# Two sets of operation prices in a scheduler that writes out the engines' order, older ones for the HGRN part

## The reference

```python
# layer 0
h = rmsnorm(x, norm_mix[0])
proj = h @ w_in                       # -> u (256) | q, f, i, g (4 x 768)
pool_out = multi_scale_causal_pool(u) # windows 2/4/8/16, minus self, a linear map per group
f = lb + (1 - lb) * sigmoid(fz); k = (1 - lb) * sigmoid(-fz); v = silu(iz)
S_t = diag(f_t) S_{t-1} + k_t outer v_t;  o_t = S_t^T q_t      # 6 heads, 128 x 128 state
o = o * rsqrt(mean(o*o) + EPS) * gain * sigmoid(gz)
x = x + concat(pool_out, o) @ w_out
x = x + square(relu(rmsnorm(x, norm_mlp[0]) @ ff_w1[0])) @ ff_w2[0]
# layer 1
bg, cg, hv = split(rmsnorm(x, norm_mix[1]) @ odd_w_in)
x = x + (bg * conv3(cg * hv)) @ odd_w_out
x = x + square(relu(rmsnorm(x, norm_mlp[1]) @ ff_w1[1])) @ ff_w2[1]
y = rmsnorm(x, norm_final)
```

## Time and profile before

| | us |
|---|---|
| median of 6 runs | 1518.09 (1514.1 to 1580.4) |
| profiled execution | 1514.85 |
| its span, slowest core | 1513.3 |
| spans of the eight cores | 1497.8 to 1513.3 |
| TensorE busy | 1416.9 (94%) |
| VectorE busy | 1078.6 (71%) |
| ScalarE busy | 849.1 (56%) |
| GpSimd busy | 219.1 (14%) |

### The profile page before, as it was taken

How to read it: one execution, slowest core, us unless ns; L and a number is a source line. 1 busy time by engine, 2 the same in 40 slices (tenths; PEclk the granted TensorE clock), 3 DMA queues, 4 the chain that set the end, 5 groups by cost and what they waited for, 6 DMA issues and landing times.

```text
span 1513.3 us, 25120 instructions; the slowest of 8 cores (1497.8 to 1513.3 us)
## 1 busy us (share of the span) xinstructions
PE 1416.9 (94%) x9189; PEld 710.7 (47%) x9189; DVE 1078.6 (71%) x1911; ACT 849.1 (56%) x1711; POOL 219.1 (14%) x286
## 2 busy tenths in 40 slices
PE   4799799989999898999999999999999999999997
PEld 2555455545445344444445544445544444443442
DVE  4689888777556768867767655557667678867767
ACT  4677668875324546945647422236746546735655
POOL 1134534433300000100100000000000000100100
PEclk9899999999999999999999999999999999999999
DMA  7855145747960534533642322300426535843642
GB/s 162 177 79 80 33 99 100 134 96 174 160 133 15 98 51 75 98 57 70 112 70 43 63 43 51 70 15 1 81 41 104 92 50 97 177 75 70 112 70 112
DMA packets 61715, 130.19 MB, mean 86 GB/s; under 512 B 6350, under 2 KB 33084, under 8 KB 61580
## 3 DMA queue, kind: packets, MB, share of 16 engines
q0 software_dynamic: 25952, 90.78, 37.1%
q1 hardware_dynamic: 34028, 37.48, 8.5%
q10 hardware_dynamic: 1616, 0.33, 0.1%
HBM read 203.86 MB, written 15.54 MB: 145 GB/s over the span
## 4 chain that ended last, share of the span: by engine, by line
PE 67%; DMA 15%; DVE 10%; ACT 4%; issue 3%; ACTq 1%; POOL 1%; SPq 0%; POOLq 0%; DVEq 0%
PE pp L549 43%; PE pp L547 21%; DMA ring<-w2w 7%; DMA ring<-wst 3%; DMA ring<-w1w 3%; PE pp L559 2%; ACT arena L495 2%; DVE arena L514 1%; DVE arena L1680 1%; DVE mixT L514 1%; DVE x_sb L526 1%; DVE x_sb L514 1%; DMA mixT<-xs 1%; DVE ring L514 1%; DMA arena<-st_conv 1%
## 5 line engine op out<-in xcount | busy, mean ns | idle before, releaser
L549 PE MATMUL pp<-hT,ring 128*128 128x512 f16 (+1 forms) x2480 | 463.1, 335 | 15.0 <-DVE ring L514 9.9
L514 DVE TENSOR_TENSOR x_sb<-x_sb,pp 128x512 f32<-128x512 f32 x488 | 321.0, 684 | 120.1 <-PE pp L547 42.1
L549 PEld LDWEIGHTS pp<-hT,ring 128*128 128x128 f16 x2480 | 202.8, 98 | 241.9 <-issue 38.7
L495 ACT ACTIVATE pp<-pp 128x512 f32<-128x512 f32 x336 | 191.6, 583 | 213.6 <-PE pp L547 184.6
L495 ACT ACTIVATE arena<-arena 128x512 f16<-128x512 f16 (+1 forms) x278 | 169.2, 624 | 46.5 <-DVE arena L1680 37.7
L549 PE MATMUL pp<-ring,mixT 128*128 128x512 f16 x824 | 191.9, 379 | 1.7 <-DVE mixT L514 1.7
L495 ACT ACTIVATE arena<-pp 128x512 f32<-128x512 f32 (+5 forms) x228 | 126.8, 562 | 118.6 <-PE pp L549 80.7
L547 PE MATMUL pp<-ring,arena 128*128 128x512 f16 x488 | 125.7, 379 | 0.0
L547 PE MATMUL pp<-hT,ring 128*128 128x512 f16 x448 | 113.2, 379 | 9.7 <-ACT pp L495 9.0
L549 PEld LDWEIGHTS pp<-ring,mixT 128*128 128x128 f16 x824 | 77.7, 98 | 89.9 <-issue 4.4
L564 POOL DMA_DIRECT2D ring<-w2w x56 | 29.5, 529 | 480.3 <-PE pp L549 187.1
(11 more groups left out here) (181 smaller groups left out, 1962.7 us busy)
## 6 DMA issues: line engine op xcount, KB each, us to landing
ring<-wst POOLq DMA_DIRECT2D x57, 512.0 KB, 8.8
ring<-w1w POOLq DMA_DIRECT2D x56, 512.0 KB, 6.6
ring<-w2w POOLq DMA_DIRECT2D x56, 512.0 KB, 6.7
x_sb<-xp SPq DMA_DIRECT2D x28, 512.0 KB, 7.8
yp<-x_sb SPq DMA_DIRECT2D x16, 512.0 KB, 2.7
x_sb<-st_hgrn SPq DMA_DIRECT2D x24, 256.0 KB, 5.8
nhs<-x_sb SPq DMA_DIRECT2D x24, 256.0 KB, 2.5
ring<-wst POOLq DMA_DIRECT2D x8, 256.0 KB, 8.1
```

The source lines that it names most:

```text
L495: return e.activation(out=out, in_=in_, func=func, bias=bias, scale=scale)
L514: return Op(eng, lambda e: e.tensor_tensor(out=out, in0=in0, in1=in1, op=op), R, W, occ, occ + 0.08)
L549: ins = e.matmul(o, l, r, start=s, stop=t)
```

## The change

A list `late` is empty at first; `main` appends to it after the flag `("S", LASTHEAD, 2)`, just ahead of the out projection of the second half. While it is empty, `ACT`, `TT`, `TS`, `STT` and `CP` use older formulas; afterwards those of before. `TT` on GpSimd has the older formula throughout. The three prices of 0.6 us by hand in the seven-product MLP are gone, so that Relu and Square there are priced by `ACT`. No operation is added or taken away by the diff.

```diff
+        late = []
...
-            occ = 0.14 + fsz(in_) / 1280.0 + (0.19 if accum is not None else 0.0)
-            if not in_psum(in_):
-                occ += 0.03
-            if (not isinstance(scale, float) or not isinstance(bias, float)) and fsz(in_) > 8:
-                occ += 0.09
+            n = fsz(in_)
+            if late:
+                occ = 0.14 + n / 1280.0 + (0.19 if accum is not None else 0.0) + (0.0 if in_psum(in_) else 0.03)
+                if (not isinstance(scale, float) or not isinstance(bias, float)) and n > 8:
+                    occ += 0.09
+            else:
+                occ = 0.17 + n / 1400.0 + (0.12 if accum is not None else 0.0)
+                if not isinstance(scale, float) or not isinstance(bias, float):
+                    occ += 0.04
...
-            ps = in_psum(in0) or in_psum(in1)
-            two = not ps and all(a.dtype in (F16, BF16) for a in (in0, in1, out))
-            occ = 0.12 + n / (1925.0 if two else 965.0) + (0.05 if not ps and not two and n > 256 else 0.0)
+            if late:
+                ps = in_psum(in0) or in_psum(in1)
+                two = not ps and all(a.dtype in (F16, BF16) for a in (in0, in1, out))
+                occ = 0.12 + n / (1925.0 if two else 965.0) + (0.05 if not ps and not two and n > 256 else 0.0)
+            else:
+                occ = 0.07 + n / (1920.0 if fast else 900.0)
             if eng == "pool":
-                occ = 0.2 + n / 480.0
+                occ = 0.15 + n / 465.0
...
-            occ = 0.134 + fsz(out) / 1800.0
+            occ = 0.134 + fsz(out) / 1800.0 if late else 0.07 + fsz(out) / 1920.0
...
-            occ = 0.184 + fsz(out) / 964.0
+            occ = 0.184 + fsz(out) / 964.0 if late else 0.1 + fsz(out) / 850.0
...
-            occ = 0.12 + fsz(out) / (1925.0 if eng == "dve" else 465.0)
+            occ = (0.12 if late else 0.07) + fsz(out) / (1925.0 if eng == "dve" else 465.0)
...
-                                yield ACT(v, v, AF.Square, B, B, t=0.6)
+                                yield ACT(v, v, AF.Square, B, B)
...
-                            yield ACT(v, bank(k), AF.Relu, [B_ps[k]], B, t=0.6)
+                            yield ACT(v, bank(k), AF.Relu, [B_ps[k]], B)
...
-                            yield ACT(v, v, AF.Square, B, B, t=0.6)
+                            yield ACT(v, v, AF.Square, B, B)
...
             yield up(("S", LASTHEAD, 2))
+            late.append(1)
             yield from outproj(1, U_WO, 1, "mix", range(8, 17))
```

## The result

The changed kernel takes 1505.7 us (median) against 1517.7 for the kernel before beside it: a ratio of 0.9914, 95% interval 0.9886 to 0.9943. That is 0.9% faster, where 0.3% was forecast, and still inside the 1% called "within". The ratio leaves out executions in which a whole die was granted a lower clock; those in which one or two pairs of neighbouring cores were, at about 0.97 of the full clock over the span, count in it. So I compare stages as means over the eight cores: the mean span goes from 1505.4 to 1499.2 us, which is 6.2 us of the medians' 12.0, as the two profiled executions lie on opposite sides of theirs.

What follows compares the result with a forecast made beforehand. TensorE was taken as the bound nearly everywhere from 212 us on, with VectorE fullest in 112 to 212. 1514.85 + 1.7 - 2.8 - 3.4 + 0 = 1510.4, on the median's scale 1513.6, rounded to 1513; range 1495 to 1535.

Steps and rivals of the forecast that it cites:

- The sign of the whole: Whole kernel: faster, 1513 us forecast against a median of 1518.09, 0.3% below.
- The start was set apart: Before 57 us: the start waits for loads, which no formula of the diff prices, so it was set apart.
- 300 to 352 us, -3.4: Late load of weights costs 6.8 us of idle time and slow matmuls; half counted as gone, -3.4 us.
- 112 to 212 us, -2.8: Order drawn anew; TensorE's idle time falls from 12.6 to 9.8 us, the share of the window before, -2.8 us.
- Hopeful prices, +1.7: HGRN part: unit prices too low by 1.99 us instead of 1.09 put matmuls ahead of their inputs, +1.7 us.
- Rival A: Unit matmuls, 57 to 424 us: hopeful plan makes TensorE stand, +20 us to 1538, idle over 40 us; chance 0.16.
- X and Y at nothing: The two seven-product MLPs: Relu and Square priced 0.05 us too hopeful, taken as 0, bounds +-7 us.
- Rival C: Before 212 us: VectorE meets GpSimd more often, longer means in its rows, +4.5 or +9 us, 1523 to 1527; chance 0.12.
- Rival B: Stops in 112 to 212 and 300 to 352 us go, 20 us faster, 1498; chance 0.22.
- Rival D: Whole kernel: the change does nothing, the order stays unchanged; chance 0.02.

Runs made afterwards that it cites:

- e1: Changed kernel with the three prices of 0.6 us for Relu and Square put back; 1501.8 us, ratio to the kernel before 0.9912.
- s1: Kernel before with the older prices only until the first unit wrote its output, about 44 us; ratio 0.9981, X start 494.1.
- f1: Kernel before, with the slot freed by the out projection given first to head 3's second weights; ratio 0.9976, X start 493.3.
- t3: Changed kernel with the older ScalarE and VectorE prices of the HGRN part times 0.8; ratio to the kernel before 1.0135.
- e2: Kernel before with only the three prices of 0.6 us for Relu and Square taken out; 1518.0 us, ratio 1.0014.
- t2: Kernel before with the scheduler's tie of 0.03 us made 0.04, no price changed; profiled execution 1522.77 us.
- t6: Changed kernel with the prices of 0.6 us put back and the tie of 0.03 us made 0.04; profiled execution 1515.5 us.
- e3: Changed kernel without the switch, so the older formulas hold to the end; ratio to the kernel before 0.9946.
- e4: Kernel before with 0.05 us added to each ScalarE and VectorE price until the switch; ratio 1.0122, X start 514.9.
- t1: Kernel before with the scheduler's tie of 0.03 us made 0.02, no price changed; profiled execution 1529.28 us.

## Why the prediction was right, and where not

**The sign of the whole** was right and the time lies in the range, by a sum that left one term out. It had -4.5 us for the HGRN part; the mean of the cores shows -8.1 at X start, and -11.1 in e1. The signs that it named came: 212 to 300 and 352 to 424 us idle by 1.7 and 2.9% on the slowest core, VectorE's work to 424 us within a few us, X some us earlier, X and Y within 7. But that the sum came near is in part luck. Its terms of 1.7, -2.8, -3.4, 0 and 0 measured 0.7, -0.8, -5.4, -5.4 (the start) and 1.9 (X and Y), and another tie alone moves X by as much as the change does.

**The start was set apart**, because "no formula of the diff prices a load". This step failed. The start also holds ScalarE's squares with a sum, which the older formula prices at 1.02 us for 1024 columns (0.17 + 1024/1400 + 0.12) and the other at 1.16 (0.14 + 0.80 + 0.19 + 0.03), and VectorE's scalings behind them. Their order, not the loads alone, held TensorE at 45.91 us; which of the changed prices moved the scaled block was not tried. The term measured -5.4 us. That 57 to 112 us takes some of it back is not shown: s1, which changes the start alone, loses 7.2 us there for 7.4.

**300 to 352 us, -3.4.** The mechanism was right: the last reader of the slot stood late, and another order freed the slot earlier and had more to do meanwhile. Measured was -5.4 (7.9 to 2.5): the term counted half of a stop that went nearly whole. The earlier slot by itself brought the landing forward by 1.2 us only; what was won is work until then, and the clock that it kept. f1 shows that this stop alone is worth about as much, 4.9 us there.

**112 to 212 us, -2.8.** TensorE's idle time fell from 13.3 to 11.1 us (mean of the cores), near the forecast. The clock was lower, 0.950 for 0.964, and with that the stretch gains 0.8 us. e1, the same order, has 11.7 us idle at 0.964 and gains 1.6, so that the new order holds the clock lower is not shown; either figure is well short of the forecast. The list of TensorE's waits in this stretch has a matmul of a unit at its head, and a pooling step, as in the earlier trace rows, only behind it:

```profile
PE pp L558 <- DVE arena L523: 3.9, 1, 3.9
PE pp L558 <- DVE x_sb L535: 3.7, 3, 1.3
```

The first of these waits ends with a product on VectorE that took 1.25 us where such products have a mean of 0.623, and GpSimd was at work beside it:

```profile
157.20 1.25 DVE L523 TENSOR_TENSOR arena<-arena,gsm 128x384 bf16<-128x384 f32 x1
```

```profile
153.03 5.01 POOL L523 TENSOR_TENSOR x_sb<-x_sb 64x526 f32<-64x526 f32 x4 [8.20 <-DVE arena L523]
```

**Hopeful prices, +1.7.** Measured +0.7 (1.2 to 1.4 and 0.9 to 1.4), but -0.3 in e1, the same order: no cost that stands clear of the spread. **Rival A** asked for over 40 us of idle time from 57 to 424; the slowest core has 23.4. Even the prices of t3, a fifth lower still, come to 36.0 us only (cores 0 to 3).

**X and Y at nothing.** X start to end is the longer part whenever the price by hand is taken out together with measured prices in X: 1008.0 (after), 1009.5 (e2) and 1009.8 us (t3), against 1003.9 to 1007.5 in the seven kernels with `t=0.6` and the old tie, whose mean is 1005.5. Their mean is 1009.1, so that is +3.6 us, inside the bounds of 7 but not nothing. It lies in the last stage: from 565 us after X start to the end these three lose 33.7, 34.2 and 35.3 us, the seven 26.7 to 30.8. The timeline of Y shows a wait of 3.1 us that these three have on all eight cores, and none of the seven on any; after, and then e1 at the same place:

```profile
1262.14 1.38 PE L558 MATMUL pp<-hT,ring 128*128 128x512 f16 x4 [3.09 <-DVE hids L523]
```

```profile
1247.77 1.03 PE L558 MATMUL pp<-hT,ring 128*128 128x512 f16 x4
```

VectorE squares the sample tokens' hidden columns in 0.17 us, but in the new order this stands at 1261.91 behind some dozen block sums:

```profile
1253.79 1.23 DVE L523 TENSOR_TENSOR mixT<-hT 128x2048 f16<-128x2048 f16 x1 [1.11 <-PE pp L556]
...
1261.91 0.17 DVE L523 TENSOR_TENSOR hids<-hids 128x32 f16<-128x32 f16 x1
```

In e1 it stands 12.6 us ahead of that matmul:

```profile
1235.17 0.17 DVE L523 TENSOR_TENSOR hids<-hids 128x32 f16<-128x32 f16 x1
```

The end of VectorE's chain releases TensorE; whether the squares themselves or a block sum just ahead of them is what TensorE needs was not tried. Nor is it tied to these prices (t2 and t6, with the price by hand and the other tie, have one of 3.2 us and rests of 1012.0 and 1010.4), or the whole of the loss: e3 loses 32.9 us in the last stage without it. The new prices also send seven more of the squares to ScalarE (221 from 480 us on, for 214), and no run separates that from the order. The price differences of 0.03 to 0.06 us alone are no more than the prediction said; an order drawn by them is. In the time of the launch this cost is too small to be told apart: e1 and the change have the same ratio.

**Rival C** did not come by the sign that the prediction gave for it. The rows that answer to the earlier trace rows have shorter means, 985 for 1369 ns, 148 for 765 and 147 for 274:

```profile
L535 DVE SCALAR_TENSOR_TENSOR x_sb<-x_sb,cfixw_s 128x512 bf16<-128x512 f32 x4 | 3.9, 985 | 0.0
...
L523 DVE TENSOR_TENSOR dcar<-x_sb 128x1 f32<-128x1 f32 x7 | 1.0, 147 | 0.0
...
L523 DVE TENSOR_TENSOR dcar<-arena 128x1 f32<-128x1 f32 x4 | 0.6, 148 | 0.0
```

Other rows of VectorE lengthened instead, before and after, on all eight cores alike:

```profile
L514 DVE TENSOR_TENSOR gsm<-arena 128x3 f32<-128x3 f32 x4 | 1.3, 322 | 0.0
...
L514 DVE TENSOR_TENSOR hT<-ssq,gcols_s 128x128 f16<-128x128 f32 x1 | 0.3, 292 | 0.0
```

```profile
L523 DVE TENSOR_TENSOR gsm<-arena 128x3 f32<-128x3 f32 x4 | 2.2, 561 | 0.0
...
L523 DVE TENSOR_TENSOR hT<-ssq,gcols_s 128x128 f16<-128x128 f32 x1 | 1.1, 1149 | 0.0
```

So some meetings of the two engines went and others came. An instruction of the same shape takes a fifth of its time when it stands elsewhere, and the neighbour on GpSimd is in the trace: one of the long subtractions of the kernel before ends as GpSimd's product ends, at 153.45 and 153.44 us.

```profile
152.29 1.16 DVE L514 TENSOR_TENSOR dcar<-arena 128x1 f32<-128x1 f32 x1
```

```profile
152.17 1.27 POOL L514 TENSOR_TENSOR arena<-arena 128x512 f32<-128x512 f32 x1
```

That fits the rule of the Trainium skill (SBUF — State Buffer, "Who interferes with whom") that the prediction named, by which the two block each other for a whole instruction; no run here took just the neighbour away. **Rival B** came half: one of its two stretches, 300 to 352 us, runs nearly freely now. **Rival D** is out, as the order changed.

**What was right for the wrong reason.** The prediction asked what prices that are more hopeful do. The runs do not show that, within a few hundredths of a microsecond, the size of the error does anything by itself: closer prices (e4) gave 514.9 us at X start, the older ones 488 to 491, the same ones with another tie 495.0, and the prices of before with other ties 488 on undisturbed cores. The older formulas are not shown to be better; they draw an order without two particular stops. The gain at the start came with them in every run that has them there and no further factor, with the tie of before and in t6 with another (28.7 to 29.7 us lost, 32.8 to 34.3 in the others). The late load also went nearly whole under the prices of before, with another tie in t2 (0.8 us lost).

## What to carry to other kernels

Where a scheduler picks by estimated start, a small change of prices is a new draw of the order: try several, and do not argue that the truer price gives the better order. Look in the profile for the few stops that differ between draws, and mend those by a rule, as the slot rule here did (6.0 us at X start), so that the next edit does not lose them. In a sum of idle times, count the granted clock with each stop, and leave no stage out because the thing it waits for carries no price: the order of what else stands there does.

## What the runs showed of the hardware

In t1 cores 0 and 4 run one order and one program. From about 200 to 350 us core 4 is granted 0.81 of the full clock, window after window, where core 0 has 1.00. Windows of 10 us, core 0 and then core 4:

```profile
180.00:190.00 10.00, 8.66 (x83) 5.50 (x83) 8.66 (x16) 8.49 (x18) 3.54 (x3) 1.00 0.31 109
200.00:210.00 10.00, 9.72 (x84) 5.71 (x82) 7.61 (x15) 7.64 (x16) 0.00 (x0) 1.00 0.31 70
290.00:300.00 10.00, 9.69 (x78) 5.48 (x77) 7.93 (x13) 8.53 (x17) 6.78 (x5) 1.00 1.00 199
```

```profile
180.00:190.00 10.00, 8.71 (x76) 5.18 (x74) 8.69 (x15) 8.65 (x18) 3.54 (x3) 1.00 0.22 71
200.00:210.00 10.00, 10.00 (x53) 4.54 (x52) 7.58 (x17) 5.34 (x12) 0.00 (x0) 0.81 0.39 81
290.00:300.00 10.00, 10.00 (x81) 6.20 (x80) 6.67 (x14) 7.16 (x14) 4.34 (x4) 0.81 0.13 34
350.00:360.00 10.00, 10.00 (x53) 4.36 (x51) 9.96 (x17) 4.47 (x9) 5.74 (x5) 0.90 0.58 173
```

Its neighbour, core 5, shows the same 0.81 from 200 to 210 us, while core 6 of the same die has 1.00; first core 5, then core 6:

```profile
200.00:210.00 10.00, 10.00 (x50) 4.39 (x49) 8.81 (x18) 5.63 (x12) 0.00 (x0) 0.81 0.49 105
```

```profile
200.00:210.00 10.00, 9.95 (x65) 5.00 (x63) 9.14 (x18) 5.98 (x14) 0.00 (x0) 1.00 0.53 112
```

Cores 4 and 5 start X at 511.3 and 513.0 us, some 24 us behind the other six. In t3 it came pair by pair too: cores 6 and 7 fell to 0.81 between 70 and 80 us, cores 4 and 5 between 90 and 100, while core 0 had 1.00. What sets it off, and why a pair, stays open. The Trainium skill (TensorE: Matmul & The Clock Gate, "Seeing it yourself") tells of a limiter that takes a whole die to 13/16 of the clock, 0.81; here two cores of a die were at 0.81 while core 6 of the same die had 1.00, so by the measurement it need not be the whole die.
